# A one-column silu at the head of the expert pass, and the last expert's result added in two halves

## The reference, cut to what matters

```python
def swiglu(h, w_gate, w_up, w_down):
    return (jax.nn.silu(h @ w_gate) * (h @ w_up)) @ w_down

def moe_swiglu(h, router_w, router_b, w_gate, w_up, w_down):
    ...
    top_vals, top_idx = lax.top_k(logits, TOP_K)
    gates = jax.nn.softmax(top_vals, axis=-1)
    combine = jnp.sum(jax.nn.one_hot(top_idx, N_EXPERTS, dtype=jnp.float32) * gates[..., None], axis=1)
    ...
    for e in range(N_EXPERTS):
        out = out + combine[:, e:e + 1] * swiglu(t, w_gate[e], w_up[e], w_down[e])
    return out.reshape(B, S, Dm)
```

## Time and profile before

| what | value |
| --- | --- |
| time, median of 3 runs | 1628.25 us (1626.71 to 1629.65) |
| time of the profiled execution | 1629.31 us |
| its span | 1627.6 us |
| PE busy | 1488.7 us (91%) |
| DVE busy | 1234.3 us (76%) |
| ACT busy | 914.7 us (56%) |
| one pass of the expert loop | 55.10 us |

### The profile page before, as it was taken

How to read it: one execution, slowest core, us unless ns; L and a number is a source line. 1 busy time by engine, 2 the same in 40 slices (tenths; PEclk the granted TensorE clock), 3 DMA queues, 4 the chain that set the end, 5 groups by cost and what they waited for, 6 DMA issues and landing times.

```text
span 1627.6 us, 19797 instructions
## 1 busy us (share of the span) xinstructions
PE 1488.7 (91%) x7242; PEld 1217.9 (75%) x7243; DVE 1234.3 (76%) x1687; ACT 914.7 (56%) x1180; POOL 4.2 (0%) x16
## 2 busy tenths in 40 slices
PE   6899989998999987988899998958799999999995
PEld 5788877786788876866788887736688788878884
DVE  4767898667668886767777875794588988888887
ACT  6546653447555644455433334555377776787774
POOL 0000000000000000000000000000000000000000
PEclk9999999999999999999899998988699999999998
DMA  8454457773344464652567683212288788889882
GB/s 331 181 211 161 172 219 273 304 263 130 130 179 183 157 256 182 251 188 78 208 257 265 236 313 124 104 52 78 80 313 314 303 337 294 316 304 333 308 317 97
DMA packets 54264, 358.16 MB, mean 220 GB/s; under 512 B 7088, under 2 KB 8112, under 8 KB 13360
## 3 DMA queue, kind: packets, MB, share of 16 engines
q1 hardware_dynamic: 51392, 353.47, 58.4%
q0 software_dynamic: 144, 2.10, 0.3%
q10 hardware_dynamic: 2656, 1.64, 0.3%
HBM read 356.13 MB, written 1.05 MB: 219 GB/s over the span
## 4 chain that ended last, share of the span: by engine, by line
PE 68%; DVE 17%; ACT 6%; issue 5%; DMA 2%; ACTq 0%; PEldq 0%; DVEq 0%; PEld 0%; SPq 0%
PE ps L422 20%; PE ps L424 20%; PE ps L423 19%; DVE wlo L1361 6%; PE ps L808 2%; ACT whi L951 2%; DMA rw<-router_dram 2%; DVE tok L1513 1%; PE ps L533 1%; DVE tok L1934 1%; PE ps L579 1%; PE ps L514 1%; DVE acc L1384 1%; DVE attn_scratch L1601 1%; ACT attn_scratch L1100 1%
## 5 line engine op out<-in xcount | busy, mean ns | idle before, releaser
L1361 DVE TENSOR_TENSOR wlo<-raw,whi 128x2048 fp32r<-128x2048 f32 (+1 forms) x303 | 651.1, 2171 | 179.3 <-ACT whi L951 166.8
L951 ACT ACTIVATE whi<-raw 128x2048 fp32r<-128x2048 f32 (+1 forms) x303 | 546.7, 1822 | 267.9 <-PE ps L424 265.7
L422 PE MATMUL ps<-whi,xhi 128*128 128x512 f32 (+3 forms) x1360 | 536.9, 395 | 25.4 <-DVE wlo L1361 16.4
L424 PE MATMUL ps<-whi,xlo 128*128 128x512 f32 (+3 forms) x1360 | 525.1, 386 | 0.0
L423 PE MATMUL ps<-wlo,xhi 128*128 128x512 f32 (+3 forms) x1360 | 524.7, 386 | 0.0
L422 PEld LDWEIGHTS ps<-whi,xhi 128*128 128x128 f32 x1360 | 259.3, 191 | 85.9 <-issue 19.2
L424 PEld LDWEIGHTS ps<-whi,xlo 128*128 128x128 f32 x1360 | 258.7, 190 | 52.5
L423 PEld LDWEIGHTS ps<-wlo,xhi 128*128 128x128 f32 x1360 | 259.6, 191 | 47.6
L422 PE MATMUL ps<-whi,ahi 128*128 128x512 f32 x440 | 178.7, 406 | 12.8 <-DVE wlo L1361 12.8
L423 PE MATMUL ps<-wlo,ahi 128*128 128x512 f32 x440 | 175.3, 398 | 0.0
L424 PE MATMUL ps<-whi,alo 128*128 128x512 f32 x440 | 175.3, 398 | 0.0
(11 more groups left out here) (247 smaller groups left out, 1168.4 us busy)
## 6 DMA issues: line engine op xcount, KB each, us to landing
raw<-stream_dram SPq DMA_DIRECT2D x318, 1024.0 KB, 5.2
raw<-stream_dram SPq DMA_DIRECT2D x30, 512.0 KB, 4.2
attn_scratch<-toep_dram POOLq DMA_DIRECT2D x1, 2048.0 KB, 9.5
raw<-stream_dram SPq DMA_DIRECT2D x2, 528.0 KB, 3.9
h<-x_dram SPq DMA_DIRECT2D x1, 1024.0 KB, 5.4
y<-tok SPq DMA_DIRECT2D x2, 512.0 KB, 2.7
head_scratch<-w_s_dram ACTq DMA_DIRECT2D x1, 512.0 KB, 18.4
gates<-fg_dram ACTq DMA_DIRECT2D x1, 512.0 KB, 21.6
```

The lines of the kernel that those rows point to most:

```text
L422: pe.matmul(o, xh, wh, start=start, stop=False)
L424: return pe.matmul(o, xl, wh, start=False, stop=stop)
L951: act.activation(whi[:, q % SPL, 0:w], raw[:, s % RAW, 0:w], ACT.Copy).then_inc(sem("hi_done"), 1)
L1361: dve.tensor_tensor(wlo[:, q % SPL, 0:w], raw[:, s % RAW, 0:w], whi[:, q % SPL, 0:w].bitcast(F32), ALU.subtract).then_inc(sem("lo_done"), 1)
```

## The change

ACT executes one more activation at the head of each pass: the silu of one column of `ones`, written into a column of `st` that nothing reads. With it the compiler places one table load per pass, ahead of this silu, where it had placed two. DVE adds the last expert's result in two halves of columns, two operations each: the first behind the second chunk (after `lo_of(0)`, ahead of the place masks), the second behind the third chunk (after `lo_of(1)`), where it had made all four between the product of the first chunk and the splits of s4 and s5. `y_added` is counted up with the second half. The call behind the loop, for the last expert, does both halves at once as before, and so does the second loop, which these inputs don't enter.

```diff
@@ -1295,6 +1295,7 @@
             take_gathered()
             with act.Fori(0, NE) as i:
                 T.loop(i, x_tr=6, x_g=2, x_y=2, x_sg=6, x_gt=1)
+                act.activation(st[:, 30:31], ones[:, 0:1], ACT.Silu)
                 for j in range(6):
                     silu(j, i)
                     if j > 0:
@@ -1925,14 +1926,15 @@
-            def add_expert(i):
-
-                for n in range(2):
+            def add_expert(i, halves=(0, 1)):
+
+                for n in halves:
                     dve.wait_ge(sem("y_psum"), T.up("x_y"))
                     for t in range(NT):
                         o = macc[:, t, n * W:(n + 1) * W]
                         m = dve.scalar_tensor_tensor(o, ps[:, (5, 7, 3, 4)[2 * n + t], :], comb[:, t, i], o, ALU.mult, ALU.add)
-                m.then_inc(sem("y_added"), 1)
+                if 1 in halves:
+                    m.then_inc(sem("y_added"), 1)
@@ -1945,10 +1947,11 @@
             with dve.Fori(0, NE) as i:
                 T.loop(i, x_xg=2, x_silu=6, x_hi=6, x_a=6, x_y=2, y_hi=1, dve=2, xg_ready=1, x_tr=0)
                 product(0, i)
-                add_expert(bass.ds(i, 1))
                 for j in range(1, 6):
                     product(j, i)
                     lo_of(j - 1)
+                    if j < 3:
+                        add_expert(bass.ds(i, 1), (j - 1,))
                     if j == 1:
```

## The result

The changed kernel takes 1633.78 us (median of 11 runs, 1633.16 to 1634.84), the kernel before in the same comparison 1629.42 (11 runs, 1626.71 to 1631.09). The ratio is 1.0027, with a 95% interval of 1.0018 to 1.0036: 4.36 us slower, where 5.3 were predicted. The profiled execution took 1633.74 us.

A forecast was written before the change was run, and what follows sets the result against it. PE at full clock sets the pace, 53.59 of 55.10 us a pass; DVE's backlog at s8 adds 0.49 in seven passes and 1.83 in the first, 5.3 us in all: 1633.5 us, range 1629.3 to 1638.7.

The forecast's parts named there:

- The fixed point: ACT's split of s5 waits for PE to leave s2, so the 1.08 us saved by the load don't move its start.
- The backlog: DVE's additions moved behind s5 make s8 late: 16.10 us from s5's whi to PE's s8, +0.49 us per pass.
- the one gap that I had to bound: DVE's gap behind a lo, ahead of the additions' first half: taken as 0.45 us, low bound 0.23.
- The second gap: DVE's gap behind a lo, ahead of the additions' second half: taken as 0.23 us.
- The tail: Behind s8 nothing takes the loss back: ACT's 2.38 us wait behind the gather and PE's before s16 move with PE.
- The rival that the loss would be swallowed there: Rival B: PE's 0.57 us idle before the last down blocks shrinks by the loss; 1628 to 1631 us, chance 0.19.
- The first pass: From s5's whi to PE's s8 14.50 us before; the new chain plus 0.23 for a longer gap gives +1.83 us.
- The sum: Whole kernel: 7 x 0.49 + 1.83 = 5.3 us slower, 1633.5 us against the median.
- the high bound of the gaps: On DVE, 0.45 us ahead of the second half and 0.45 left ahead of the masks: +0.67 a pass, +5.4.
- the range: Forecast kernel time from 1629.3 to 1638.7 us, meant to take in both bounds of the gaps.
- the one-column silu: On ACT at the pass head, delays the s2 and s3 splits by 0.20 us, covered by 0.43 before PE takes s2.

## Why the prediction was right

**The fixed point.** That the split of s5 waits for PE to leave s2, and that the saved load therefore reaches nobody, was the step on which all hung. It held: the idle time in front of it grew from 0.57 to 1.91, and the kernel without the silu is no faster and no slower.

**The backlog.** Predicted from the start of s5's whi to PE's s8: 16.10 us; measured 1303.00 - 1287.00 = 16.00. The missing 0.10 is the one gap that I had to bound: 0.33 us ahead of the first half, where I took 0.45. The second gap was 0.23 and that ahead of the masks 0, both as taken. So a pass grew by 0.43 instead of 0.49. DVE's idle time was 0.68 (0.6 predicted), the waits before s6 and s8 that PE's starts show are 0.72 and 0.98 (0.8 and 0.95).

**The tail.** It moved with PE, as the wait of 2.38 us behind the gather had said; no part of the 0.43 came back. ACT behind the gather and PE before s16, in the changed kernel's third pass:

```profile
1315.65 0.39 ACT L1284 ACTIVATE ahi<-ps 128x256 fp32r<-128x256 f32 x1 [2.38 <-PE ps L851]
1327.50 0.50 PE L422 MATMUL ps<-whi,ahi 128*128 128x512 f32 x1 [0.57 <-DVE wlo L1362]
```

Both waits are as long as before. The rival that the loss would be swallowed there is out.

**The first pass.** From its split of s5 to s8 it took 1191.94 - 1175.93 = 16.01 us instead of 14.50: 1.51 more, where 1.83 were predicted. I had added 0.23 for the longer gap of that pass (0.68), and that did not come; it was 0.34. These two rows of the first pass, of ACT and of PE, answer to the earlier trace rows:

```profile
1175.93 1.92 ACT L951 ACTIVATE whi<-raw 128x2048 fp32r<-128x2048 f32 x1 [2.31 <-PE ps L424]
1191.94 0.50 PE L422 MATMUL ps<-whi,xhi 128*128 128x512 f32 x1 [0.73 <-DVE wlo L1362]
```

**The sum.** 7 x 0.43 + 1.51 = 4.5 us, against 4.4 in the spans and in the medians. The two spans also differ by 0.21 us up to the first s5 and by 0.3 the other way behind the loop, which nearly cancel and are no part of the forecast. The term that was mis-sized is the gap ahead of the first half, in the first pass most. A slip without weight: the high bound of the gaps adds up to 1638.9, and the range, said to take it in, ends at 1638.7.

What the prediction had too large without harm is the one-column silu, at 0.20 instead of 0.11; it was hidden ahead of s2 in any case.

**What stays open.** The gap between the lo and the masks is 0.45 us (0.68 in the first pass) in the two kernels with all four additions in their old place, the kernel before and the one with the silu only. It is 0.33 in the kernels that have the masks there with fewer additions ahead of s4, though the program's own lines at that place are the same. No run here tells why.

## What to carry to other kernels

A wait that a change removes is worth something only up to the next instruction whose start another engine fixes. Find that point in the timeline first, here the split of a block into the buffer that PE has not left yet. Work moved from in front of it to behind it is added to what follows (DVE's way from s5 to s8 takes 11.71 us instead of 9.18, with 2.63 us of additions more in it), and the time in front of it that nothing else fills turns into idle time (0.68 us). Side work of an engine that runs ahead of PE belongs in front of such a point as far as it fits, and the rest where that engine idles anyway, but ahead of the instruction that waits for it.

## What the runs showed of the hardware

A table load costs its 1.28 us and 0.01 to 0.02 at its ends, nothing more: 1277.91 for a copy that ended at 1277.90, and 1279.21 for the activation behind it. The 1.38 us of drain that the Trainium skill adds (ScalarE: Activation LUTs, "What ACT_TABLE_LOAD costs") are at none of the loads in the expert loop of either kernel.

A one-column activation ahead of a long one costs 0.11 us, not its own 0.20, since the two overlap.

In the first pass the changed kernel's PE started 1.71 us later than before (1164.23, before 1162.52), and yet its split of s5 came just 0.21 later. In the window from 1163 to 1168 its granted clock was 0.66 on average, before 0.50, that is 1.2 GHz throughout. The change is not what did it. From PE's start in the loop to the split of s5 it took 13.20 us in the profiled execution of the kernel before and 13.21 in that of the kernel with one addition before s5, which has the silu and the moved additions and also a clock of 0.50 in this window. In the eight others it took 11.7 to 11.8, in those with the moved additions only (1163.79 to 1175.50) and with the silu only (1163.90 to 1175.60) too. What decides between the two is not shown. Such a difference of 1.5 us lies within the spread of the kernel before alone, 4.4 us over its runs.
